# A two-block transformer kernel: the second mixer's steps in a woven order, and row tile 1 turned later

## What is computed

```python
for l in range(DEPTH_2):      # hybrid_layer, written out
    x = x + 0.5 * swiglu_2(rmsnorm(x, ffn1_norm[l]), ...)
    x = x + mixer(rmsnorm(x, mix_norm[l]), w_in[l], ...) @ w_out[l]
    x = x + 0.5 * swiglu_2(rmsnorm(x, ffn2_norm[l]), ...)
```

## Time and profile before

| | us |
|---|---|
| median of 3 runs | 1962.02 (1957.16 to 1966.44) |
| the profiled execution | 1965.11, its span 1963.3 |
| TensorE busy | 1941.2 (99%), 13125 matmuls |
| VectorE, ScalarE busy | 1196.9 (61%), 1013.3 (52%) |
| fills, 677 of them, busy | 99.3 in the page's group, which counts overlapping ends once |

### The profile page before, as it was taken

One profiled execution on the slowest core, in us unless ns is written; L12 is line 12 of the kernel. 1 busy time (PEld: TensorE's weight loads), 2 busy tenths in 40 slices (PEclk: granted clock), 3 DMA queues, 4 the chain that ended last, 5 costly groups with the idle time before them and its releaser, 6 DMA issues.

```text
span 1963.3 us, 31921 instructions
## 1 busy us (share of the span) xinstructions
PE 1941.2 (99%) x13125; PEld 1658.7 (84%) x13125; DVE 1196.9 (61%) x2463; ACT 1013.3 (52%) x2044; POOL 91.4 (5%) x187
## 2 busy tenths in 40 slices
PE   9999999999999999999999999999999999999998
PEld 7888889888888788888888887888888888888887
DVE  5676556756454566766665745567556757455565
ACT  5565555423222555645655565456555645655554
POOL 0000001111210000010001000000000000000000
PEclk9999999999898999999999999999999999999999
DMA  6564542221202455635562333556355623334553
GB/s 231 192 235 183 178 145 108 87 93 47 69 29 71 161 193 196 233 105 192 200 228 83 108 118 108 174 190 252 113 179 206 237 98 111 104 143 140 189 183 122
DMA packets 42721, 296.19 MB, mean 151 GB/s; under 512 B 4832, under 2 KB 4960, under 8 KB 10576
## 3 DMA queue, kind: packets, MB, share of 16 engines
q1 hardware_dynamic: 41184, 288.32, 41.3%
q0 software_dynamic: 1392, 5.83, 0.9%
HBM read 293.08 MB, written 1.05 MB: 150 GB/s over the span
## 4 chain that ended last, share of the span: by engine, by line
PE 93%; DVE 3%; ACT 2%; POOL 1%; issue 0%; DMA 0%; POOLq 0%; DVEq 0%; ACTq 0%
PE PS L1507 21%; PE PS L1449 16%; PE PS L1451 14%; PE PS L1450 14%; PE PS L1509 10%; PE PS L1458 4%; PE PS L1722 1%; PE PS L1741 1%; PE PS L1946 1%; PE PS L1734 1%; PE PS L1484 1%; PE PS L1858 1%; PE PS L1910 1%; PE PS L1638 1%; PE PS L1935 1%; PE PS L1902 1%
## 5 line engine op out<-in xcount | busy, mean ns | idle before, releaser
L2334 DVE TENSOR_TENSOR wlo<-raw,whi 128x512 fp32r<-128x512 f32 (+4 forms) x780 | 616.8, 833 | 189.8 <-ACT whi L1983 184.2
L1507 PE MATMUL PS<-xhl,whi 128*128 128x512 f32 x1728 | 613.4, 399 | 0.0
L1983 ACT ACTIVATE whi<-raw 128x512 fp32r<-128x512 f32 (+4 forms) x780 | 534.8, 739 | 123.6 <-PE PS L1451 121.3
L1509 PE MATMUL PS<-xhl,wlo 128*128 128x256 f32 x1728 | 485.0, 281 | 0.0
L1507 PEld LDWEIGHTS PS<-xhl,whi 128*128 128x128 f32 x1728 | 324.7, 188 | 79.4
L1509 PEld LDWEIGHTS PS<-xhl,wlo 128*128 128x128 f32 x1728 | 326.3, 189 | 2.1
L1449 PE MATMUL PS<-whi,yh 128*128 128x512 f32 (+2 forms) x580 | 228.3, 394 | 0.5 <-DVE small L2555 0.2
L1451 PE MATMUL PS<-whi,yl 128*128 128x512 f32 (+2 forms) x580 | 225.0, 388 | 0.0
L1450 PE MATMUL PS<-wlo,yh 128*128 128x512 f32 (+2 forms) x580 | 224.8, 388 | 0.0
L1449 PE MATMUL PS<-whi,xhl 128*128 128x512 f32 (+4 forms) x480 | 192.8, 402 | 0.5
L2419 DVE TENSOR_TENSOR arena<-arena,PS 128x256 f32<-128x256 f32 x216 | 90.2, 418 | 159.1 <-ACT arena L2053 159.1
(11 more groups left out here) (269 smaller groups left out, 2590.4 us busy)
## 6 DMA issues: line engine op xcount, KB each, us to landing
raw<-wall SPq DMA_DIRECT2D x249, 1024.0 KB, 4.9
raw<-wall SPq DMA_DIRECT2D x12, 768.0 KB, 4.3
raw<-wall SPq DMA_DIRECT2D x8, 968.0 KB, 4.8
raw<-wall SPq DMA_DIRECT2D x4, 896.0 KB, 5.0
arena<-ebias POOLq DMA_DIRECT2D x2, 768.0 KB, 4.6
raw<-wall SPq DMA_DIRECT2D x2, 720.0 KB, 4.0
raw<-wall SPq DMA_DIRECT2D x2, 640.0 KB, 3.8
X<-x SPq DMA_DIRECT2D x2, 512.0 KB, 5.4
```

The costliest lines, as they stand in the source:

```text
L1507: e.matmul(b, hi[:, c0:c0 + 128], xhl[:, k, :, :].rearrange("p a t -> p (a t)"), start=(k == 0), stop=False, skip_group_check=True)
L1509: p = e.matmul(b[:, 0:256], lo[:, c0:c0 + 128], xh[:, k, :], start=False, stop=(k == 7), skip_group_check=True)
L1983: e.activation(whi[slot_of(i)][:, c].bitcast(F32R), raw[i % 3][:, c], copy).then_inc(*M.sig("whi", ("split", i, q)))
L2334: e.tensor_tensor(wlo[slot_of(i)][:, c], raw[i % 3][:, c], whi[slot_of(i)][:, c].bitcast(F32), ALU.subtract).then_inc(*M.sig("wlo", *[("ha ...
```

## The change

It adds costs for the second mixer's steps to PACE, writes mix2's order with woven() instead of together(), with rest 0.5 and each attention unit a chain of its own instead of six at a time behind group c, moves the turn of row tile 1 behind six k steps in all stages, and has another table of fills. The table's keys are steps, its values numbers of fills; it adds up to 267, 26, 192 and 192 fills in stages 1, 4, 5 and 8 before, and 242, 26, 120 and 118 after. The order of mix1 is written as before but for the turn.

```diff
@@ -119,6 +119,15 @@
+    "turn_iq": (("pe", 0.45), ("act", 0.6)), "turn_ik": (("pe", 0.15), ("act", 0.4)), "ix_score": (("pe", 0.4), ("act", 0.55)),
+    "ix_sum": (("pe", 2.5), ("act", 0.35)), "lat_turn": (("pe", 0.25), ("act", 0.9), ("dve", 0.5)),
+    "latent_up": (("pe", 1.0), ("act", 0.45)), "turn_c": (("pe", 0.35), ("act", 0.6)), "u_score_c": (("pe", 0.25), ("dve", 0.4)),
...
+    "ix_rope": (("dve", 2.8),), "ix_diag": (("dve", 1.2),), "ix_top": (("dve", 1.5),), "krope": (("dve", 1.2),),
+    "ix_mask": (("dve", 0.7),), "brope": (("dve", 1.9),), "qrope": (("dve", 1.4),), "u_norm": (("dve", 0.7),),
@@ -126,24 +135,21 @@
 BLANKS = {
-    ('turn_x', 1, 0, 0): 6, ('turn_x', 1, 1, 0): 8, ('proj', 1, 'qkv', 1, 0): 5, ('proj', 1, 'gate', 0, 0): 14,
-    ('proj', 1, 'gate', 0, 4): 2, ('att_turn', 1, 0, 0, 0): 13, ('turn_ao', 1): 3, ('up', 1, 0, 0, 0): 12,
-    ('shift_mm', 1, ('v', 1), 0, 0): 17, ('r_s', 1, 1, 2): 4, ('r_mean', 1, 1): 19, ('r_d', 1, 2, 4): 10,
-    ('r_x', 1, 2, 5): 3, ('r_d', 1, 2, 5): 4, ('r_rp', 1, 2): 3, ('r_s', 1, 2, 3): 11, ('r_lora', 1, 6): 3,
-    ('r_g0', 1, 5): 3, ('r_d', 1, 4, 5): 5, ('r_d', 1, 5, 3): 4, ('r_yp', 1, 4): 2, ('r_s', 1, 5, 2): 10,
-    ('r_s', 1, 5, 3): 4, ('r_x', 1, 6, 2): 5, ('r_d', 1, 6, 3): 7, ('r_x', 1, 7, 5): 5, ('r_d', 1, 7, 5): 3,
...
-    ('wo', 1, 2, 0, 0): 5, ('wo', 1, 2, 1, 0): 2, ('proj', 4, 'gh', 0, 0): 26, ('turn_x', 5, 0, 0): 6,
-    ('turn_x', 5, 1, 0): 9, ('turn_iq', 5): 19, ('proj', 5, 'in2', 2, 4): 9, ('lat_turn', 5, 0, 0): 13,
-    ('latent_up', 5, 'ukv', 0, 0): 18, ('proj', 5, 'in2', 3, 0): 38, ('turn_c', 5, 0): 4,
-    ('u_turn', 5, 'c', 0, 0): 4, ('turn_b', 5, 0): 11, ('u_out', 5, 'a', 0, 0): 7, ('wout2', 5, 2, 0, 0): 10,
-    ('u_out', 5, 'a', 4, 1): 14, ('turn_out', 5, 2): 8, ('wout2', 5, 1, 0, 0): 9, ('wout2', 5, 0, 0, 0): 11,
-    ('wout2', 5, 0, 1, 0): 2, ('turn_x', 8, 0, 0): 6, ('turn_x', 8, 1, 0): 9, ('turn_iq', 8): 19,
...
+    ('turn_x', 1, 0, 0): 6, ('proj', 1, 'qkv', 1, 0): 5, ('proj', 1, 'gate', 0, 0): 14,
+    ('proj', 1, 'gate', 0, 4): 2, ('att_turn', 1, 0, 0, 0): 13, ('turn_ao', 1): 3, ('up', 1, 0, 0, 0): 14,
+    ('shift_mm', 1, ('v', 1), 0, 0): 18, ('r_s', 1, 1, 2): 5, ('r_d', 1, 2, 4): 11, ('r_x', 1, 2, 5): 4,
+    ('r_d', 1, 2, 5): 4, ('r_rp', 1, 2): 4, ('r_s', 1, 2, 3): 11, ('r_g0', 1, 5): 3, ('r_d', 1, 4, 5): 7,
+    ('r_d', 1, 5, 3): 4, ('r_s', 1, 5, 2): 10, ('r_s', 1, 5, 3): 4, ('r_x', 1, 6, 2): 7, ('r_d', 1, 7, 5): 4,
...
+    ('turn_x', 5, 0, 0): 6, ('ix_score', 5, 0, 0): 2, ('latent_up', 5, 'uq', 0, 0): 20,
+    ('latent_up', 5, 'ukv', 0, 0): 16, ('proj', 5, 'in2', 3, 4): 17, ('proj', 5, 'in2', 4, 4): 9,
+    ('turn_out', 5, 4): 6, ('wout2', 5, 2, 0, 0): 11, ('turn_out', 5, 2): 8, ('wout2', 5, 1, 0, 0): 11,
+    ('wout2', 5, 0, 0, 0): 12, ('wout2', 5, 0, 1, 0): 2, ('turn_x', 8, 0, 0): 6, ('ix_score', 8, 0, 0): 2,
...
 }
@@ -553,7 +559,7 @@
-            if lead and (k, tt) == (3 if s else 5, 0):
+            if lead and (k, tt) == (5, 0):
                 self.turn_half(s, 1)
                 self.feed()
@@ -999,12 +1005,6 @@
-        def units():
-            while "c" not in made:
-                yield 1
-            yield from staggered((unit(kind, h, tt, n) for kind, n in (("c", 5), ("b", 5), ("a", 6))
-                                  for tt in range(2) for h in range(n)), 6)
-
@@ -1121,7 +1121,8 @@
-        together(products(), index(), latent(), sparse(), near(), units())
+        units = [unit(kind, h, tt, n) for kind, n in (("c", 5), ("b", 5), ("a", 6)) for tt in range(2) for h in range(n)]
+        self.woven(products(), 0.5, index(), latent(), sparse(), near(), *units)
```

More of the change, by code:

```diff
@@ L121 @@
     "att_out": (("pe", 1.0), ("dve", 0.5)), "up": (("pe", 1.4),), "r_turn2": (("pe", 0.25),), "r_fin": (("dve", 1.3), ("act", 0.4), ("dve", 0.4)), "wout": (("pe", 1.4),),
+    "turn_iq": (("pe", 0.45), ("act", 0.6)), "turn_ik": (("pe", 0.15), ("act", 0.4)), "ix_score": (("pe", 0.4), ("act", 0.55)),
+    "ix_sum": (("pe", 2.5), ("act", 0.35)), "lat_turn": (("pe", 0.25), ("act", 0.9), ("dve", 0.5)),
+    "latent_up": (("pe", 1.0), ("act", 0.45)), "turn_c": (("pe", 0.35), ("act", 0.6)), "u_score_c": (("pe", 0.25), ("dve", 0.4)),
+    "u_score_b": (("pe", 0.6), ("dve", 0.4)), "u_score_a": (("pe", 0.6), ("dve", 0.4)), "u_soft": (("act", 0.45),),
+    "u_turn": (("pe", 0.2), ("act", 0.35)), "u_out": (("pe", 0.35),), "turn_b": (("pe", 0.45), ("act", 0.6)),
+    "turn_a": (("pe", 0.45), ("act", 0.6)), "turn_out": (("pe", 0.4), ("act", 0.75), ("dve", 0.5)), "wout2": (("pe", 1.4),),
+    "in2_out": (("act", 0.6),), "lat_sq": (("act", 1.9),), "lat_scale": (("dve", 0.75), ("act", 1.1)), "bias8": (("act", 1.5),),
+    "ix_rope": (("dve", 2.8),), "ix_diag": (("dve", 1.2),), "ix_top": (("dve", 1.5),), "krope": (("dve", 1.2),),
+    "ix_mask": (("dve", 0.7),), "brope": (("dve", 1.9),), "qrope": (("dve", 1.4),), "u_norm": (("dve", 0.7),),
     "proj": (("pe", 0.7),), "proj_out": (("dve", 0.7), ("act", 0.6)),
@@ L134 @@
-    ('r_s', 1, 5, 3): 4, ('r_x', 1, 6, 2): 5, ('r_d', 1, 6, 3): 7, ('r_x', 1, 7, 5): 5, ('r_d', 1, 7, 5): 3,
-    ('r_rp', 1, 7): 7, ('r_s', 1, 7, 1): 2, ('r_s', 1, 7, 2): 3, ('r_s', 1, 7, 3): 3, ('r_mean', 1, 7): 5,
-    ('r_var', 1, 7): 8, ('r_turn2', 1, 7): 6, ('turn_merged', 1, 0): 35, ('wo', 1, 1, 0, 0): 6,
-    ('wo', 1, 2, 0, 0): 5, ('wo', 1, 2, 1, 0): 2, ('proj', 4, 'gh', 0, 0): 26, ('turn_x', 5, 0, 0): 6,
-    ('turn_x', 5, 1, 0): 9, ('turn_iq', 5): 19, ('proj', 5, 'in2', 2, 4): 9, ('lat_turn', 5, 0, 0): 13,
@@ L139 @@
-    ('latent_up', 5, 'ukv', 0, 0): 18, ('proj', 5, 'in2', 3, 0): 38, ('turn_c', 5, 0): 4,
-    ('u_turn', 5, 'c', 0, 0): 4, ('turn_b', 5, 0): 11, ('u_out', 5, 'a', 0, 0): 7, ('wout2', 5, 2, 0, 0): 10,
-    ('u_out', 5, 'a', 4, 1): 14, ('turn_out', 5, 2): 8, ('wout2', 5, 1, 0, 0): 9, ('wout2', 5, 0, 0, 0): 11,
-    ('wout2', 5, 0, 1, 0): 2, ('turn_x', 8, 0, 0): 6, ('turn_x', 8, 1, 0): 9, ('turn_iq', 8): 19,
-    ('proj', 8, 'in2', 2, 4): 9, ('lat_turn', 8, 0, 0): 13, ('latent_up', 8, 'ukv', 0, 0): 18,
@@ L144 @@
-    ('proj', 8, 'in2', 3, 0): 38, ('turn_c', 8, 0): 4, ('u_turn', 8, 'c', 0, 0): 4, ('turn_b', 8, 0): 11,
-    ('u_out', 8, 'a', 0, 0): 7, ('wout2', 8, 2, 0, 0): 10, ('u_out', 8, 'a', 4, 1): 14, ('turn_out', 8, 2): 8,
-    ('wout2', 8, 1, 0, 0): 9, ('wout2', 8, 0, 0, 0): 11, ('wout2', 8, 0, 1, 0): 2,
+    ('turn_x', 1, 0, 0): 6, ('proj', 1, 'qkv', 1, 0): 5, ('proj', 1, 'gate', 0, 0): 14,
+    ('proj', 1, 'gate', 0, 4): 2, ('att_turn', 1, 0, 0, 0): 13, ('turn_ao', 1): 3, ('up', 1, 0, 0, 0): 14,
@@ new lines @@
+    ('shift_mm', 1, ('v', 1), 0, 0): 18, ('r_s', 1, 1, 2): 5, ('r_d', 1, 2, 4): 11, ('r_x', 1, 2, 5): 4,
+    ('r_d', 1, 2, 5): 4, ('r_rp', 1, 2): 4, ('r_s', 1, 2, 3): 11, ('r_g0', 1, 5): 3, ('r_d', 1, 4, 5): 7,
+    ('r_d', 1, 5, 3): 4, ('r_s', 1, 5, 2): 10, ('r_s', 1, 5, 3): 4, ('r_x', 1, 6, 2): 7, ('r_d', 1, 7, 5): 4,
+    ('r_rp', 1, 7): 7, ('r_s', 1, 7, 1): 2, ('r_s', 1, 7, 2): 3, ('r_s', 1, 7, 3): 3, ('r_mean', 1, 7): 5,
+    ('r_var', 1, 7): 10, ('r_turn2', 1, 7): 7, ('turn_merged', 1, 0): 34, ('turn_merged', 1, 4): 5,
@@ new lines @@
+    ('wo', 1, 1, 0, 0): 6, ('wo', 1, 2, 0, 0): 5, ('wo', 1, 2, 1, 0): 2, ('proj', 4, 'gh', 0, 0): 26,
+    ('turn_x', 5, 0, 0): 6, ('ix_score', 5, 0, 0): 2, ('latent_up', 5, 'uq', 0, 0): 20,
+    ('latent_up', 5, 'ukv', 0, 0): 16, ('proj', 5, 'in2', 3, 4): 17, ('proj', 5, 'in2', 4, 4): 9,
+    ('turn_out', 5, 4): 6, ('wout2', 5, 2, 0, 0): 11, ('turn_out', 5, 2): 8, ('wout2', 5, 1, 0, 0): 11,
+    ('wout2', 5, 0, 0, 0): 12, ('wout2', 5, 0, 1, 0): 2, ('turn_x', 8, 0, 0): 6, ('ix_score', 8, 0, 0): 2,
@@ L147 @@
+    ('latent_up', 8, 'uq', 0, 0): 20, ('latent_up', 8, 'ukv', 0, 0): 16, ('proj', 8, 'in2', 3, 4): 17,
+    ('proj', 8, 'in2', 4, 4): 9, ('turn_out', 8, 4): 4, ('wout2', 8, 2, 0, 0): 11, ('turn_out', 8, 2): 8,
+    ('wout2', 8, 1, 0, 0): 11, ('wout2', 8, 0, 0, 0): 12, ('wout2', 8, 0, 1, 0): 2,
 }
```

## The result

The changed kernel took 1943.62 us (median of 4 runs, 1941.83 to 1945.21); the kernel before, run beside it on the same chip, 1963.03 us (4 runs). The ratio is 0.991 (95% interval 0.989 to 0.993). The forecast was 1940 us with a range of 1928 to 1952.

A forecast was written before the change was run, and what follows sets the result against it. TensorE's own queue was taken as the bound. Weave 15.4, turn 6.5, first mixer's fills 2.0, less small waits 2.0, make 21.9 us off 1965.1, giving 1943.2; as that run was 3.1 above the median, 1940 us, range 1928 to 1952.

The forecast's parts named there:

- What bounds it: Whole kernel: only TensorE's own queue sets the time, busy 99% of the span and carrying 93% of the chain.
- The turn: Lead tiles: turning row tile 1 behind six k steps removes waits of 3.4 us and fills of 3.1 us, 6.5 us.
- The weave: Second mixers, stages 5 and 8: the woven order drops 128 fills of 0.12 us, 15.4 us gained.
- small waits: Second mixers: waits too short for a fill, small before at 0.27 us, cost 1 us more each, 2 us in all.
- The fills are the waits: TensorE's queue: fills stand where it would wait; 192 of them are 23.0 of a second mixer's 173 us.
- The first mixer's fills: Stage 1: 17 fills fewer net besides the turn, 19 dropped at r_mean, gain 2.0 us, bounds 0 and 4.
- The clock: Second mixers: 1.00 throughout, sum unchanged; rival: one fall in each costs up to 10.3 us, 1961 us, chance 0.06.
- named signs: Second mixers: 120 and 118 fills, stage 155 to 165 us instead of 173, idle under 2 us, clock 1.00.
- Short waits: Rival: the weave leaves many short waits, 7.7 us for both mixers, 1948 us; sign over 3 us idle; chance 0.14.
- No effect of the weave: Rival: the new order waits as much as before, only the turns gain, 1956 us, chance 0.03.
- Slower: Rival: a b unit before the last turn_c blocks VectorE, up to 18 us a mixer, 1976 us, chance 0.04.

The follow-up runs named there:

- the part alone: The kernel before with row tile 1 turned behind six k steps in all stages and without that turn's 26 fills: 1955.45 us, ratio 0.9969.
- fills on a free bank: The changed kernel with 14 fills added in both second mixers before the score of unit (a, 2, 1): 1941.19 us, ratio 0.9882.

## Why the prediction was right, point by point

**What bounds it: right.** 171 fills fewer on TensorE, the other engines as before, and the time fell with TensorE's own work.

**The turn: right.** In stage 2 the transposes now start 0.23 us behind the matmul before, as told:

```profile
662.84 0.39 PE L1452 MATMUL PS<-early,xhl 128*128 128x512 f32 x1
663.07 1.03 PE L1485 MATMUL PS<-C,GATE 128*128 128x128 f32 x8
```

The four stages lost 0.77 to 0.95 us against 0.86, stage 4 0.13 against none, and the part alone 6.1 to 6.9 us against 6.5.

**The weave: right in its direction, mis-sized twice, in opposite directions, and not all of it order.** The term was 128 fills less 2.0 us of small waits, 13.4 us. With the clock at 1.00 (the kernel with fills on a free bank beside the turn alone) the second mixers went from 173.47 to 164.78 and from 173.56 to 164.43 us, 17.8 us in all. What I had left out shows in the distances from start to start, added up by shape over stage 5 in both traces. The recorded fills went from 22.5 to 16.5 us; the 84 transposes of arena tiles (128x128) from 11.2 to 9.7, the 22 short products of 64x128 from 4.6 to 2.9, the 96 products of 128x384 from 19.8 to 18.7, while the 96 products of 65 columns grew from 9.1 to 10.3 us. These matmuls are the same in number and shape in both, so short waits lay hidden beneath the modelled tails of real matmuls, where neither the fills nor the idle time of 0.27 us shows them, and the weave shortened these as well. "The fills are the waits" was too strong too: of 23.0 us of fills, 16.6 show as waiting once they are out, so a part of this term (an estimated 5 us, above) is the table's and not the order's. The step that failed is "what is not in the fills are waits too short for one. Before they are small": they were not small before, and they fell instead of growing. Against that stands the unfilled wait of 1.8 us in each mixer, inside the 0 to 3 us that I had allowed, but with a consequence that I hadn't: 17.1 us of low clock that cost 6.2 us.

**The first mixer's fills: right at the place, not resolved in the whole.** At r_mean 1.2 us came free against 1.6. What I overlooked is that the fills were also holding the clock there: it fell behind r_mean in seven of eight profiles without them and in none of five with them. The sum of 2.0 us agrees with the estimate at a full clock (1.7 to 2.9) and is far inside what the first mixer's clock does by itself (455.4 to 461.7 us over the seven profiles of this same part).

**The clock: the term that I put at nothing.** The forecast said 1.00 in the second mixers; it was 0.99 and 0.96. With it, two more of the named signs failed: the idle time was 2.65 and 2.80 us instead of under 2, and stage 8 was longer than 165 us by either cut. As a rival it had 0.06 and 10.3 us a mixer. What came was that rival at a third of its size, on top of a weave that was better by 4.4 us. The sum came out 3.6 us from the measurement because the two nearly cancelled, and that is luck. By the equal-clock column, 27 us were gained and 8 given back.

**The other rivals.** Short waits (1948 us): TensorE is idle for 2.65 and 2.80 us, close to the 3 us that would have spoken for it, but in one place and not in many. No effect of the weave (1956): excluded by the stages' 8.6 and 5.3 us. Slower (a unit of group b ahead of turn_c, 1976 us): no wait of that kind is among TensorE's waits, and both mixers got shorter.
